# A hybrid decoder trunk on one core: seams between stages reordered, first weight tile ahead of x, a layer's first eight units over eight banks, per-layer gate kept in PSUM, output in four transfers

## The chip, the cores and the metric

One NeuronCore of a Trainium2 chip runs the whole program. The metric is the device time in microseconds from the first to the last instruction of one execution, the median over several runs.

## The reference

One inference step of two layers over 288 tokens (a prompt of 256, and 8 samples of 4), width 1024, all in float32. Each layer:

```python
z = rmsnorm(x, ln1) @ w_in                    # [u, v | B, C, xin | gate_A, gate_B], 7 x 1024
v = rmsnorm(gelu(v), ln_v)
ya = (gelu(u) * (tril(w_s[g]) @ v + b_s[g])) @ w_a
yb = (B * conv3_causal(C * xin)) @ w_b
x += (sigmoid(gate_A) * ya + sigmoid(gate_B) * yb) @ w_o
# PEER: q = rmsnorm(x, ln2) @ w_q; 8 heads, top 16 of 128 x 128 key pairs, softmax weights g
#   x += sum_k g_k * gelu(u_tab[eid_k] . h) * v_tab[eid_k]        over 16384 experts
x += sigmoid(rmsnorm(x, ln3) @ w_pg) * (pe @ w_ple)
```

At the end comes one more RMSNorm. Beside y, the outputs are the convolution state and the normalised v rows of the samples.

## The kernel before

**Units.** Activations lie feature-major: x is 8 chunks of 128 features by 288 tokens. Every weight comes from one stream of tiles [128, 1024] (512 KB); four tiles are a quad, and a layer has `QUADS` of them. One tile makes one unit: TensorE multiplies its 8 blocks of 128 x 128 with the 8 chunks of the operand and sums in one PSUM bank. Precision comes from a split in three: weight and operand are each a high part (fp32r) and a low part (the rest), and a unit has 8 x 3 = 24 matmuls (high x high, high x low, low x high; lines 1326 to 1328). The stages by their first quad are v, u, c, x, b, ga, gb (0 to 13), W_a (14), W_b (16), W_o (18), W_q (20), the expert table u (24, `Q_U`, 128 units on the prompt's 256 tokens), the table v (`Q_V`, 128 units), W_ple (one quad) and W_pg, the gate (two quads, `Q_PG`).

**Queues.** Each engine runs an order written out by hand, tied together by counting semaphores. SP issues the weight tiles into four buffers `raw`, and a tile's buffer is free when its low part was made (`lo`). ScalarE makes the high part (`split` in its block, line 463), VectorE the low part (`ahead`, line 832), both two units ahead of TensorE, since `w_hi` and `w_lo` have two buffers. In the expert stage for u GpSimd makes the low part in halves (line 380). So one late step holds the next-but-one unit.

**Banks.** A unit j of a quad writes bank j (0 to 3), and VectorE or ScalarE evacuates it (`evac`); TensorE waits for the bank's evacuation before the next quad's unit j. Bank 4 is for the sum of squares. Normalisation is applied late: the product is made from x times the gain, and `evacuate` (line 878) multiplies it with `root`, 1/rms of each token.

**Sums of squares.** ScalarE squares the chunks (line 444), GpSimd adds eight chunks with seven additions (`sum_chunks`, line 304), TensorE sums over the partitions with a float32 matmul of a matrix of ones (`sum_squares`, line 1316) after the second unit of the stage's first quad (`first_quad`), ScalarE takes the square root (`mean_root`, line 502, with a table load ahead at line 497) and VectorE the reciprocal (`inverse_root`, line 854). There are four in a layer, and one at the end.

**From W_b to W_o.** VectorE's loop evacuates a W_b unit into t_op (line 966), makes a weight low part (967), adds the other branch (969), and makes the operand's low part (971) after ScalarE's high part (607).

**Experts.** During the u units 0 to 63 (quads 0 to 15, `U_TOP` 13 and `U_ONLY` 3; `fine_segment`) VectorE picks the top 16 with sorts and makes `route`. TensorE transposes it after quad 14 (`rt_w`, `rT_ok`, lines 1446 to 1454). VectorE turns it into `routeT` (lines 1084 to 1096, `rT_in`); ScalarE waits for that ahead of quad 15 (line 655), and in quad 15 also writes ones to `mat` (`one_tiles`, line 646), whose end is `ones_ok`. For the last 64 units (`mixing_quad`) VectorE makes one-hot matrices of four tokens at a time (`matches`, `shared`, lines 1103 and 1110), ScalarE their low halves (`low_halves`, line 665), TensorE multiplies them (lines 1476, 1477) between the units' chunks, the first group after 21 of unit 0's 24 matmuls.

**The gate.** VectorE evacuates W_pg's product times root to `z[8 + c]`, ScalarE takes the sigmoid in place (line 774), VectorE multiplies with `z[c]` (1272), adds to x (1276) and, with ScalarE (`next_operand`), makes the next layer's operand (`next_lower`, line 871). Then all engines jump back to the head of the layer's loop.

**The end.** VectorE makes t_op in eight products (line 1304), and GpSimd sends y_out in two halves (line 429).

## Time and profile before

| | us |
|---|---|
| median of 3 runs | 2337.24 (2336.13 to 2341.18) |
| the profiled execution's own time | 2335.74 |
| its span, first to last instruction | 2334.2 |
| TensorE, matmuls busy | 2268.6 |
| VectorE busy | 1708.1 |
| ScalarE busy | 1390.2 |
| GpSimd busy | 875.9 |

The profile is of one execution. Its own time stands 1.5 us under the median. PE is TensorE's matmuls, PEld its weight loads, DVE VectorE, ACT ScalarE, POOL GpSimd and SP the queue that issues the weights. Matmuls overlap, so a busy time is the sum of overlapping stretches merged, and the distance from one start to the next says how fast they flow: 0.133 us for a matmul of 288 columns and 0.119 us for one of 256 in an undisturbed unit. A row of a timeline has its start, its length, engine, line, operation, output and inputs, shapes and count, and in brackets how long the engine had been idle before it and whose signal is taken to have ended that.

### The profile page before, as it was taken

What the parts mean: (1) busy time and instruction counts of PE and PEld (TensorE: products, weight loads), DVE (VectorE), ACT (ScalarE), POOL (GpSimd) and SP (SyncE); (2) the same over time, 40 slices, a digit from 0 to 9 for tenths busy, and PEclk for the clock granted to TensorE, in tenths of its full rate; (3) what the DMA queues carried; (4) which work ended last, traced back from release to release, by engine and by line L of the source; (5) the groups of instructions that cost most, each with busy time, mean ns of one, the idle gap of its engine ahead of it and who ended that gap; (6) DMA issues with size and microseconds to landing.
All of it is one profiled execution on the core that took longest, in us unless ns stands there. A gap on an engine that the chain in (4) does not pass through costs nothing.

```text
span 2334.2 us, 52338 instructions
## 1 busy us (share of the span) xinstructions
PE 2268.6 (97%) x15806; PEld 2103.0 (90%) x15806; DVE 1708.1 (73%) x3261; ACT 1390.2 (60%) x2712; POOL 875.9 (38%) x789
## 2 busy tenths in 40 slices
PE   7999999999999999999999999999999999999996
PEld 7989999998999888888899999999999998888885
DVE  5536768956888788788764467699378878888877
ACT  5544446666777555555654444566677775555555
POOL 3100007986777222111221001099877761211112
PEclk9999999999999999999999999999999999999998
DMA  5434454554444789788444345455444448888873
GB/s 185 155 121 170 158 182 153 183 180 160 156 159 154 254 294 321 268 298 279 165 156 155 119 166 182 134 185 185 165 160 159 155 158 285 295 311 278 295 255 102
DMA packets 126650, 460.77 MB, mean 197 GB/s; under 512 B 14672, under 2 KB 14864, under 8 KB 126032
## 3 DMA queue, kind: packets, MB, share of 16 engines
q1 hardware_dynamic: 105840, 384.02, 46.8%
q0 software_dynamic: 20704, 75.52, 11.5%
q8 instruction: 44, 0.72, 0.1%
q14 instruction: 62, 0.51, 0.1%
HBM read 455.53 MB, written 3.95 MB: 197 GB/s over the span
## 4 chain that ended last, share of the span: by engine, by line
PE 69%; POOL 11%; issue 11%; DVE 4%; ACT 2%; POOLq 1%; DVEq 0%; ACTq 0%; DMA 0%; SPq 0%
PE ps L1326 13%; PE ps L1328 12%; PE ps L1327 12%; POOL w_lo L380 11%; PE ps L1500 9%; PE ps L1502 9%; PE ps L1501 9%; PE ps L1476 1%; PE ps L1477 1%; ACT w_hi L463 1%; DVE w_lo L832 1%; DVE b_lo L871 1%; POOLq L306 1%; PE ps L1385 0%; ACT b_hi L506 0%
## 5 line engine op out<-in xcount | busy, mean ns | idle before, releaser
L1326 PE MATMUL ps<-h_hi,w_hi 128*128 128x256 f32 (+1 forms) x2592 | 752.2, 290 | 26.5 <-DVE w_lo L815 12.0
L380 POOL TENSOR_TENSOR w_lo<-raw,w_hi 128x512 fp32r<-128x512 f32 x508 | 649.2, 1292 | 281.9 <-ACT w_hi L485 153.0
L1327 PE MATMUL ps<-h_lo,w_hi 128*128 128x256 f32 (+1 forms) x2592 | 743.1, 287 | 0.0
L1328 PE MATMUL ps<-h_hi,w_lo 128*128 128x256 f32 (+1 forms) x2592 | 739.1, 285 | 0.0
L1326 PEld LDWEIGHTS ps<-h_hi,w_hi 128*128 128x128 f32 x2592 | 494.0, 191 | 30.2 <-issue 18.9
L1327 PEld LDWEIGHTS ps<-h_lo,w_hi 128*128 128x128 f32 x2592 | 493.4, 190 | 0.1
L1328 PEld LDWEIGHTS ps<-h_hi,w_lo 128*128 128x128 f32 x2592 | 490.9, 189 | 0.0
L463 ACT ACTIVATE w_hi<-raw 128x1024 fp32r<-128x1024 f32 x340 | 359.7, 1058 | 198.0 <-PE ps L1328 193.3
L1173 DVE TENSOR_TENSOR w_lo<-raw,w_hi 128x512 fp32r<-128x512 f32 x504 | 348.1, 691 | 127.8 <-ACT w_hi L703 86.0
L832 DVE TENSOR_TENSOR w_lo<-raw,w_hi 128x1024 fp32r<-128x1024 f32 x214 | 264.1, 1235 | 219.4 <-ACT w_hi L463 216.9
L1500 PE MATMUL ps<-w_hi,h_hi 128*128 128x512 f32 x1016 | 401.5, 395 | 0.0
L1502 PE MATMUL ps<-w_hi,h_lo 128*128 128x512 f32 x1016 | 400.0, 394 | 0.0
L1501 PE MATMUL ps<-w_lo,h_hi 128*128 128x512 f32 x1016 | 398.2, 392 | 0.0
L1326 PE MATMUL ps<-b_hi,w_hi 128*128 128x288 f32 x1152 | 345.5, 300 | 6.3 <-DVE w_lo L832 4.2
L1328 PE MATMUL ps<-b_hi,w_lo 128*128 128x288 f32 x1152 | 341.4, 296 | 0.0
L1327 PE MATMUL ps<-b_lo,w_hi 128*128 128x288 f32 x1152 | 336.2, 292 | 0.0
L703 ACT ACTIVATE w_hi<-raw 128x512 fp32r<-128x512 f32 x248 | 156.9, 633 | 199.6 <-PE ps L1502 192.7
L1502 PEld LDWEIGHTS ps<-w_hi,h_lo 128*128 128x128 f32 x1016 | 191.2, 188 | 45.4
L1501 PEld LDWEIGHTS ps<-w_lo,h_hi 128*128 128x128 f32 x1016 | 191.4, 188 | 43.9
L1500 PEld LDWEIGHTS ps<-w_hi,h_hi 128*128 128x128 f32 x1016 | 190.7, 188 | 43.4 <-issue 0.8
L1326 PEld LDWEIGHTS ps<-b_hi,w_hi 128*128 128x128 f32 x1152 | 216.4, 188 | 11.0 <-issue 5.2
L1327 PEld LDWEIGHTS ps<-b_lo,w_hi 128*128 128x128 f32 x1152 | 219.3, 190 | 0.3
(214 smaller groups left out, 3031.5 us busy)
## 6 DMA issues: line engine op xcount, KB each, us to landing
raw<-stream SPq DMA_DIRECT2D x730, 512.0 KB
x_keep<-x POOLq DMA_DIRECT2D x2, 1152.0 KB, 6.4
x<-x_keep POOLq DMA_DIRECT2D x2, 1152.0 KB, 10.3
x<-x_in SPq DMA_DIRECT2D x4, 288.0 KB, 3.9
y_out<-t_op POOLq DMA_DIRECT2D x2, 576.0 KB, 3.1
ws<-ws_in POOLq DMA_DIRECT2D x2, 512.0 KB, 3.6
ring<-u_rows,rows POOLq DMA_INDIRECT x44
ring<-stream,rows POOLq DMA_INDIRECT x42
```

The costliest lines, as they stand in the source:

```text
L306: pool.drain()
L380: return pool.tensor_tensor(w_lo[:, k % 2, lo_col:hi_col], raw[:, k, lo_col:hi_col], w_hi[:, k % 2, lo_col:hi_col].bitcast(F32), ALU.subtract)
L463: act.activation(w_hi[:, j % 2, :], raw[:, j, :], ACT.Copy).then_inc(hi, 1)
L703: act.activation(w_hi[:, k % 2, 0:D // 2], raw[:, k, 0:D // 2], ACT.Copy).then_inc(v_hi, 1)
L832: dve.tensor_tensor(w_lo[:, j % 2, :], raw[:, j, :], w_hi[:, j % 2, :].bitcast(F32), ALU.subtract).then_inc(lo, 1)
L1173: dve.tensor_tensor(w_lo[:, k % 2, at:at + D // 2], raw[:, k, at:at + D // 2], w_hi[:, k % 2, at:at + D // 2].bitcast(F32), ALU.subtract). ...
L1326: pe.matmul(out, wh, rhs_hi, start=first, stop=False)
L1327: pe.matmul(out, wh, rhs_lo, start=False, stop=False)
L1328: return pe.matmul(out, wl, rhs_hi, start=False, stop=last)
L1500: pe.matmul(out, m_up, wh, start=first, stop=False)
L1501: pe.matmul(out, m_up, wl, start=False, stop=False)
L1502: m = pe.matmul(out, m_low, wh, start=False, stop=last)
```

## The change

- SP issues the first weight tile ahead of x, the other three behind it; ScalarE runs a Copy on a spare element first, splits tile 0 ahead of the operand and tile 1 behind it; VectorE makes tile 0's low part ahead of the operand's low parts.
- `sum_chunks` adds six chunks (five additions). `sum_squares` multiplies three inputs with ones: the sum, and the last two squares. In a layer's first quad it stands after the third unit.
- The first eight units write the banks of `V_BANK` (0, 1, 2, 3, 5, 6, 7, 4); their evacuation and the steps of ScalarE and VectorE are written in a new order.
- W_b: the addition stands ahead of the weight's low part. W_q's first quad: the third tile's low part stands ahead of the second evacuation.
- The route is transposed after quad 13. ScalarE waits for the transposition alone ahead of quad 15, and makes group 0's low halves within quad 15, in its third step. VectorE makes the first one-hot matrices ahead of waiting for `ones_ok`. `share` is copied ahead of `rt_w`.
- The gate: VectorE scales the product in its bank, ScalarE's sigmoid and VectorE's multiplication stay there, x is added from there; the bank is given free by ScalarE at `next_operand`. The order of splits, gates and operand parts changes, and the tile for the next layer's second unit comes last.
- The output goes in four transfers from SP's queue.

```diff
--- before.py
+++ after.py
@@ -54 @@
...
+V_BANK = [0, 1, 2, 3, 5, 6, 7, 4]
@@ -210 @@
...
+scaled = sem("scaled")
@@ -270 @@
...
+    sp.dma_start(raw[:, 0, :], quads[0, 0]).then_inc(raw_in[0], 16)
...
-    for j in range(4):
+    for j in range(1, 4):
@@ -284 @@
...
+    for c in range(0, C, 2):
+        sp.wait_ge(t_ok, DEPTH * T_OPS + c + 2)
+        sp.dma_start(y_out[:, c:c + 2, :], t_op[:, c:c + 2, :]).then_inc(out_y, 16)
@@ -299 @@
...
-        for k in range(1, C):
+        for k in range(1, C - 2):
...
-            if k < C - 1:
+            if k < C - 3:
@@ -424 @@
...
-    for half in range(2):
-        pool.wait_ge(t_ok, DEPTH * T_OPS + (half + 1) * (C // 2))
-        pool.dma_start(y_out[:, half * (C // 2):(half + 1) * (C // 2), :],
-                       t_op[:, half * (C // 2):(half + 1) * (C // 2), :]).then_inc(out_y, 16)
...
-    pool.wait_ge(out_y, 32)
+    pool.wait_ge(out_y, 16 * C // 2)
@@ -444 @@
...
+    act.activation(spare[:, :], eps[:, :], ACT.Copy)
+    act.wait_ge(raw_in[0], 16)
+    act.activation(w_hi[:, 0, :], raw[:, 0, :], ACT.Copy).then_inc(hi, 1)
...
-    for j in range(2):
-        act.wait_ge(raw_in[j], 16)
-        act.activation(w_hi[:, j, :], raw[:, j, :], ACT.Copy).then_inc(hi, 1)
+    act.wait_ge(raw_in[1], 16)
+    act.activation(w_hi[:, 1, :], raw[:, 1, :], ACT.Copy).then_inc(hi, 1)
@@ -490 @@
...
-                        beside(i * 4 + j)
+                        beside(i * 4 + j, j)
@@ -529 @@
...
-        step(0, 0)
-        step(0, 1)
+        for n in range(3):
+            step(0, n)
         mean_root(1)
-        gelu(0)
-        gelu(1)
-        for j in (2, 3):
-            step(0, j)
-            gelu(j)
-        for j in range(4):
-            step(1, j)
-            gelu(4 + j)
+        for n in range(3, 8):
+            step(n // 4, n % 4)
+            gelu(n - 3)
+        for n in range(5, 8):
+            gelu(n)
@@ -647 @@
...
-        fine_segment(1, U_TOP - 1, lambda u: one_tiles(u + (KEYS - 4 * U_TOP), 1))
+        fine_segment(1, U_TOP - 1, lambda u, j: one_tiles(u + (KEYS - 4 * U_TOP), 1))
...
-        act.wait_ge(rT_in, L + 1)
+        act.wait_ge(rT_ok, L + 1)
...
-        fine_segment(U_TOP + U_ONLY - 1, 1,
-                     lambda u: one_tiles((u - (E_MIX - 4)) * below + E_MIX, below))
-        act.drain().then_inc(ones_ok, 1)
@@ -671 @@
...
-        low_halves(0, 0, range(GROUP))
+        def rest_of_ones(u, j):
+            if j == 2:
+                act.wait_ge(rT_in, L + 1)
+                low_halves(0, 0, range(GROUP))
+            one_tiles((u - (E_MIX - 4)) * below + E_MIX, below)
+        fine_segment(U_TOP + U_ONLY - 1, 1, rest_of_ones)
+        act.drain().then_inc(ones_ok, 1)
@@ -770 @@
...
-            emptied(4 * (Q_PG - KEYS // 4) + c)
-            act.activation(z[:, 8 + c, :], z[:, 8 + c, :], ACT.Sigmoid).then_inc(sig, 1)
+            act.wait_ge(scaled, L * C + (c + 1))
+            act.activation(ps[:, c % 4, 0:T], ps[:, c % 4, 0:T], ACT.Sigmoid).then_inc(sig, 1)
...
+            act.nop().then_inc(evac, 1)
...
+        step(Q_PG, 2)
...
-        for c in range(2, C):
-            step(Q_PG + c // 4, c % 4)
+        next_operand(0)
+        step(Q_PG, 3)
+        sigmoid(2)
+        next_operand(1)
+        step(Q_PG + 1, 0)
+        sigmoid(3)
+        sigmoid(4)
+        next_operand(2)
+        for c in range(5, C):
+            step(Q_PG + 1, c - 4)
@@ -804 @@
...
+    def first_lower(j):
+        dve.wait_ge(hi, j + 1)
+        dve.tensor_tensor(w_lo[:, j, :], raw[:, j, :], w_hi[:, j, :].bitcast(F32),
+                          ALU.subtract).then_inc(lo, 1)
+    first_lower(0)
...
-    for j in range(2):
-        dve.wait_ge(hi, j + 1)
-        dve.tensor_tensor(w_lo[:, j, :], raw[:, j, :], w_hi[:, j, :].bitcast(F32),
-                          ALU.subtract).then_inc(lo, 1)
+    first_lower(1)
@@ -878 @@
...
-        ahead(0, 0)
-        ahead(0, 1)
+        def first_v(n):
+            dve.wait_ge(mm, u0 + (n + 1))
+            dve.tensor_tensor(z[:, n, :], ps[:, V_BANK[n], 0:T], root[:, :], ALU.mult).then_inc(evac, 1)
+        for n in range(3):
+            ahead(0, n)
         inverse_root(1)
-        evacuate(0, 0, z[:, 0, :], root[:, :])
-        evacuate(0, 1, z[:, 1, :], root[:, :])
-        for n in range(2, 8):
-            evacuate(n // 4, n % 4, z[:, n, :], root[:, :])
-            ahead(n // 4, n % 4)
+        first_v(0)
+        ahead(0, 3)
+        first_v(1)
+        first_v(2)
+        ahead(1, 0)
+        first_v(3)
+        first_v(4)
+        for n in range(5, 8):
+            ahead(1, n - 4)
+            first_v(n)
@@ -964 @@
...
-                ahead(i + Q_B, j)
...
+                ahead(i + Q_B, j)
@@ -980 @@
...
+        ahead(Q_Q, 2)
         evacuate(Q_Q, 1, z[:, 1, :], root[:, :])
-        for j in (2, 3):
-            evacuate(Q_Q, j, z[:, j, :], root[:, :])
-            ahead(Q_Q, j)
+        evacuate(Q_Q, 2, z[:, 2, :], root[:, :])
+        evacuate(Q_Q, 3, z[:, 3, :], root[:, :])
+        ahead(Q_Q, 3)
@@ -1077 @@
...
+        dve.drain()
+        dve.tensor_copy(share[:, :], flat(route[:, 2, 0:S_BLOCKS, :]))
         dve.drain().then_inc(rt_w, 1)
-        dve.tensor_copy(share[:, :], flat(route[:, 2, 0:S_BLOCKS, :]))
@@ -1132 @@
...
-        dve.wait_ge(ones_ok, L + 1)
-        dve.sem_inc(passed, 1)
-        evacuated(Q_U + U_TOP + U_ONLY)
...
+        dve.wait_ge(ones_ok, L + 1)
+        dve.sem_inc(passed, 1)
+        evacuated(Q_U + U_TOP + U_ONLY)
+        dve.sem_inc(passed, 1)
@@ -1267 @@
...
+        def scale(c):
+            dve.wait_ge(mm, u0 + (Q_PG * 4 + c + 1))
+            dve.tensor_tensor(ps[:, c % 4, 0:T], ps[:, c % 4, 0:T], root[:, :], ALU.mult).then_inc(scaled, 1)
...
-            dve.tensor_tensor(z[:, 8 + c, :], z[:, 8 + c, :], z[:, c, :], ALU.mult).then_inc(plus, 1)
+            dve.tensor_tensor(ps[:, c % 4, 0:T], ps[:, c % 4, 0:T], z[:, c, :], ALU.mult).then_inc(plus, 1)
...
-            dve.tensor_tensor(x[:, c, :], x[:, c, :], z[:, 8 + c, :], ALU.add).then_inc(x_up, 1)
+            dve.tensor_tensor(x[:, c, :], x[:, c, :], ps[:, c % 4, 0:T], ALU.add).then_inc(x_up, 1)
@@ -1281 @@
...
-        for c in range(C):
-            evacuate(Q_PG + c // 4, c % 4, z[:, 8 + c, :], root[:, :])
-            if c >= 2:
-                ahead(Q_PG + c // 4, c % 4)
-            if c >= 1:
-                gate(c - 1)
-            if c >= 3:
-                next_lower(c - 3)
-            if c >= 1:
-                add_gated(c - 1)
+        scale(0)
+        scale(1)
+        ahead(Q_PG, 2)
+        gate(0)
+        add_gated(0)
+        scale(2)
+        gate(1)
+        add_gated(1)
+        next_lower(0)
+        for c in (3, 4):
+            scale(c)
+            ahead(Q_PG + c // 4, c % 4)
+            gate(c - 1)
+            add_gated(c - 1)
+            next_lower(c - 2)
+        for c in (5, 6):
+            scale(c)
+            gate(c - 1)
+            add_gated(c - 1)
+            ahead(Q_PG + c // 4, c % 4)
+            next_lower(c - 2)
+        scale(C - 1)
+        gate(C - 2)
+        add_gated(C - 2)
+        gate(C - 1)
+        add_gated(C - 1)
         next_lower(C - 3)
-        gate(C - 1)
         next_lower(C - 2)
-        add_gated(C - 1)
         next_lower(C - 1)
+        ahead(Q_PG + 1, 3)
@@ -1310 @@
...
-    def sum_squares(n, acc=0):
+    def sum_squares(n):
...
-        pe.matmul(ps[:, 4, 0:T], ones[:, :], sq[:, acc, :], start=True, stop=True).then_inc(ss_ok, 1)
+        pe.matmul(ps[:, 4, 0:T], ones[:, :], sq[:, 0, :], start=True, stop=False)
+        pe.wait_ge(sq_ok, n * C)
+        pe.matmul(ps[:, 4, 0:T], ones[:, :], sq[:, C - 2, :], start=False, stop=False)
+        pe.matmul(ps[:, 4, 0:T], ones[:, :], sq[:, C - 1, :], start=False, stop=True).then_inc(ss_ok, 1)
@@ -1346 @@
...
-                       order=range(C), until=(0, 0, 0, 0)):
+                       order=range(C), until=(0, 0, 0, 0), squares_at=1):
@@ -1358 @@
...
-                if j == 1 and squares is not None:
-                    sum_squares(L * NORMS + squares, order[0])
-        first_quad(0, 0, squares=1)
-        segment(1, 3)
+                if j == squares_at and squares is not None:
+                    sum_squares(L * NORMS + squares)
+        first_quad(0, 0, squares=1, squares_at=2)
+        for j in range(4):
+            pe.wait_ge(lo, u0 + (4 + j + 1))
+            if j == 3:
+                pe.wait_ge(evac, e0 + 5)
+            for c in range(C):
+                m = product(ps[:, V_BANK[4 + j], 0:T], j, c * P, h_hi[:, c, :], h_lo[:, c, :],
+                            c == 0, c == C - 1)
+            m.then_inc(mm, 1)
+        segment(2, 2)
@@ -1443 @@
...
-        fine_segment(0, U_TOP + U_ONLY - 1)
+        fine_segment(0, U_TOP + 1)
@@ -1451 @@
...
-        fine_segment(U_TOP + U_ONLY - 1, 1)
+        fine_segment(U_TOP + 1, U_ONLY - 1)
```

## Rows read from the trace of the kernel before

**Rows 1.** The page's busy times: engine, busy us (share) x instructions
```profile
PE 2268.6 (97%) x15806; PEld 2103.0 (90%) x15806; DVE 1708.1 (73%) x3261; ACT 1390.2 (60%) x2712; POOL 875.9 (38%) x789
```
**Rows 2.** Waits of PE, whole span: line <- releaser: total us, times, longest us
```profile
PE ps L1326 <- DVE w_lo L815: 12.0, 1, 12.0
PE ps L1316 <- POOL ext L304: 11.9, 3, 8.3
PE ps L1326 <- DVE w_lo L832: 7.5, 12, 1.5
PE ps L1476 <- ACT hot_a L665: 6.2, 2, 3.1
```
**Rows 3.** Windows: length, busy of PE, PEld, DVE, ACT, POOL, clock, DMA share, GB/s
```profile
1689.90:1693.30 3.40, 3.40 (x18) 3.40 (x17) 0.00 (x0) 2.45 (x5) 3.40 (x4) 0.50 0.46 153
1703.50:1707.00 3.50, 3.50 (x19) 3.50 (x19) 2.85 (x4) 2.59 (x7) 1.73 (x2) 0.51 0.42 162
```
**Rows 4.** Timelines of ACT and PE, from the start to unit 2
```profile
10.76 1.06 ACT L453 ACTIVATE w_hi<-raw 128x1024 fp32r<-128x1024 f32 x1 [0.23 <-DMA raw<-stream]
...
17.98 1.28 ACT L463 ACT_TABLE_LOAD   x1 [3.49 <-PE ps L1328]
...
17.24 0.35 PE L1326 MATMUL ps<-h_hi,w_hi 128*128 128x288 f32 x1
...
21.72 0.40 PE L1326 MATMUL ps<-h_hi,w_hi 128*128 128x288 f32 x1 [0.19 <-DVE w_lo L832]
```
**Rows 5.** Timeline of PE, layer 0's second sum of squares
```profile
75.44 0.65 PE L1316 MATMUL ps<-ext,ones 128*128 128x288 f32 x2
...
76.06 0.29 PE L1327 MATMUL ps<-b_lo,w_hi 128*128 128x288 f32 x1
```
**Rows 6.** Timeline of PE, last chunk of W_o's first unit, layer 0
```profile
269.44 0.29 PE L1328 MATMUL ps<-h_hi,w_lo 128*128 128x288 f32 x1
271.22 0.40 PE L1326 MATMUL ps<-h_hi,w_hi 128*128 128x288 f32 x1 [1.49 <-DVE h_lo L865]
```
**Rows 7.** Timeline of PE, W_q's second quad, layer 0
```profile
308.93 0.39 PE L1326 MATMUL ps<-b_hi,w_hi 128*128 128x288 f32 x1 [0.69 <-DVE w_lo L832]
```
**Rows 8.** Timelines of PE, DVE and ACT, quad 15 and the mixing stage's entry, layer 0
```profile
537.72 0.39 PE L1326 MATMUL ps<-h_hi,w_hi 128*128 128x256 f32 x1 [1.79 <-POOL w_lo L380]
...
545.82 1.23 DVE L1103 TENSOR_TENSOR hot_a<-ps,routeT 128x1024 f16<-128x1024 f32 x1 [10.51 <-ACTq L660]
...
548.81 1.28 ACT L665 ACTIVATE hot_a<-hot_a,routeT 128x128 f16<-128x128 f16 x4 [3.23 <-DVE hot_a L1110]
...
549.27 0.23 PE L1476 MATMUL ps<-hot_a 128*128 128x128 f16 x1 [3.08 <-ACT hot_a L665]
```
**Rows 9.** Groups by form: shapes, count | busy us, mean ns | idle before, releasers
```profile
L832 DVE TENSOR_TENSOR w_lo<-raw,w_hi 128x1024 fp32r<-128x1024 f32 x214 | 264.1, 1235 | 219.4 <-ACT w_hi L463 216.9 <-issue 0.3
...
L878 DVE TENSOR_TENSOR z<-ps,root 128x288 f32<-128x288 f32 x48 | 20.9, 453 | 14.6 <-PE ps L1328 14.0 <-issue 0.3
...
L871 DVE SCALAR_TENSOR_TENSOR h_lo<-x,gains,h_hi 128x288 fp32r<-128x288 f32 x16 | 13.0, 814 | 1.6 <-ACT h_hi L506 1.6
...
L1272 DVE TENSOR_TENSOR z<-z 128x288 f32<-128x288 f32 x16 | 7.2, 450 | 0.3
```
**Rows 10.** Timelines of POOL and PE, gate and layer's end, layer 0
```profile
1139.21 1.63 POOL L304 TENSOR_TENSOR ext<-ext 128x288 f32<-128x288 f32 x2 [0.20 <-issue]
...
1140.89 0.75 PE L1316 MATMUL ps<-ext,ones 128*128 128x288 f32 x2 [1.81 <-POOL ext L304]
...
1162.80 0.39 PE L1326 MATMUL ps<-h_hi,w_hi 128*128 128x288 f32 x1 [1.95 <-DVE z L878]
...
1168.62 0.40 PE L1326 MATMUL ps<-h_hi,w_hi 128*128 128x288 f32 x1 [1.21 <-DVE h_lo L871]
```
**Rows 11.** Timelines of ACT and POOL, the end
```profile
2323.69 0.50 ACT L794 ACTIVATE root<-ps,eps 128x288 f32<-128x288 f32 x1 [0.77 <-PE ps L1316]
...
2330.10 0.56 POOL L429 DMA_DIRECT2D y_out<-t_op  x1 [1.14 <-DVE t_op L1304]
```

## The prediction

> **What bounds the kernel now.** I read the page's busy times first, then TensorE's waits, then the granted clock, and only then the timelines around each wait. TensorE is busy 97% of the 2334.2 us span [rows 1]. Its work hardly changes here, so what can be won lies in the stretches in which it stands still. The waits [rows 2] say how little that is: 12.0 us before the first matmul, 11.9 us at three sums of squares (8.3 of them in the last one), 7.5 us in twelve waits for low weight parts (the longest, 1.5 us, at 28 us, before the fifth unit of layer 0), 6.2 us at the two entries to the mixing stage. The granted clock adds something that no wait shows: four stretches of 3.41 us inside the kernel run at half speed, beginning at 549.8, 1164.2, 1689.9 and 1703.5 us, two of which stand as rows [rows 3]. A matmul-filled stretch at half speed loses half its length, 1.7 us. Each began after TensorE had stood still for 2 us or more.
>
> The profiled execution took 2335.74 us with a span of 2334.2 us; the median of the runs shown is 2337.24 us, 1.5 us above it. The sum below is against the profiled execution, and is then put on the median. From no change, about 0.2% (4.7 us) can be told here.
>
> **Start.** The first weight tile (512 KB) now goes ahead of x. Until now the second tile's split waited for its transfer until 10.76, and TensorE began after 12.0 us, behind the first tile's low part [rows 2, 4]. With the tile first, I put its landing near 5.3 us; with 1.06 us for the high part and 1.23 us for the low one TensorE begins near 8.3 us. But the second tile lands no earlier, because the bytes ahead of it are the same; ScalarE then does eight squares, loads a table (1.28 us, behind the wait for unit 0's end, at 17.98 until now) and only then splits tile three. Until now, from that load to the start of unit 2 at 21.72 it took 3.74 us [rows 4]. ScalarE is free at 14.45, so unit 2 starts at 18.2: **3.5 us** earlier, though unit 1 has already ended near 17.1. That the slow first stretch (up to 17.24, [rows 4]) comes earlier too is in these numbers. Next is the fifth unit's wait of 1.5 us [rows 2]: it goes, as units 4 to 6 have banks 5, 6 and 7, and the split that it waited for stands ahead of the root. In its place come two more matmuls for the sum (below, 1.0 us) and the 0.2 us at 21.72 is gone. Total at unit 4: **-3.7 us**. Bounds: -2.0, if table load and split fall later, to -4.7, if the stall ahead of unit 2 is nil.
>
> **Sums of squares.** Each of the nine sums has two float32 matmuls more and two GpSimd additions fewer. One sum's two passes began at 75.44, and the second weight matmul behind it at 76.06, of whose 0.62 us the first weight matmul takes 0.133 [rows 5]: a float32 matmul of 288 columns costs 0.49 us, two more 0.98 us. At the second sum (v's square sum) of either layer nothing hides them, since the additions are long done: **+2.0 us** together. Lower bound 0.7 a sum, upper 1.3, from 0.33 and 0.65 us per matmul, half and all of the pair's recorded length [rows 5]. The others are counted in their places.
>
> **W_b to W_o.** The last chunk of the first W_o unit waits 1.49 us as the profile counts it, 1.65 us over the normal distance [rows 6]. VectorE evacuates, lowers a weight tile (1.23 us, [rows 9]), and only then adds. With the addition first, the path is evacuation 0.45, addition 0.45, then the tile, while ScalarE makes the high part, then 0.45: ready 3.0 us after the unit's end where 2.8 is needed. **-1.35 us a layer, -2.7 in all**; bounds -1.65 and 0 a layer.
>
> **W_q.** The wait of 0.69 us counted, 0.86 over the distance [rows 7], is for a tile behind three evacuations; it now stands ahead of two of them, and the sum's 0.98 us gives TensorE's needs more time still. So 0.86 goes and 0.98 comes: **+0.2 us in all**, bounds -0.5 and +1.0.
>
> **Into the mixing stage.** Until now TensorE turned the routes only after quad 14; VectorE worked on them for 5 us while ScalarE stood waiting for it, so quad 15's third unit began 1.79 us late at 537.72. Then VectorE's first comparisons waited for ScalarE's last ones tile (done 545.6), ScalarE's low halves began at 548.81 and TensorE stood 3.08 us until 549.27 [rows 8]. Now the turn comes a quad earlier (11.4 us), so everything that depends on it is done before quad 15, and the comparisons no longer wait for the tiles. Over the distances the two waits are 1.94 and 3.24 us. What is new is 1.2 us of low halves in ScalarE's third step of quad 15; until now it does a step in some 2.3 us of 2.85, so it falls behind by about 0.6 and the next half tile is still in time. GpSimd then does two gathers (2.3 us) and its next half tile comes some 0.3 us late. So -5.2 + 0.3 a layer. The half-speed stretches at 549.8, 1689.9 and 1703.5, which follow exactly these waits [rows 3], have no cause any more: -5.1. **-14.9 us in all.** Bounds: -19 would need the clock to gain elsewhere too; I take -16, and -7 if both layers keep half of the waits and two of the stretches.
>
> **Gate, layer's end, next layer.** The sum waits for GpSimd until 1140.89; its last two additions took 1.63 us from 1139.21 and are dropped [rows 10]. The sum starts 1.8 us earlier and takes 1.0 us longer: unit 2 gains 0.8. The root gains nothing, since ScalarE's split and table load alone take until 1141.68. Now each product stays in its bank until gate and addition are done. VectorE does scale, gate, add (0.45 each), a tile (1.23) and an operand part (0.81 on average, [rows 9]) per unit, 3.4 us with handing over, against 3.19 for TensorE's unit. Unit 4 waits 0.8 us for its bank, unit 7 0.5 to 1.4 us for its tile, so the quads end 0.8 to 1.5 us later than until now. In return the layer's last operands come earlier: eight squares and operands follow at once, where until now the last chunk came 1.21 us after need at 1168.62. At the layer's start TensorE idles about 2 us before 1162.80 [rows 10]. The profile names VectorE's evacuation there, but that ended 0.6 us before, and the interval looks like the jump back of the outer loop; I let it stand. From there: unit 0 without a stall, unit 1 0.3 to 0.7 us for its tile, unit 2 at 1171 to 1172 instead of 1174, and no bank wait at unit 4: **-1.9 us** between the layers, bounds +3 and -4.
>
> A rule against this part: by the Trainium skill (VectorE: DVE Perf Modes, The TRN2 errata) a VectorE operation from PSUM has 120 fixed cycles instead of 58. With 0.96 GHz, an estimate from that page gives 0.065 us more for each of some 24 operations a layer, so 3 us less gain. The trace has 453 ns for the product read from PSUM and 450 ns for the one in SBUF [rows 9], and the measurement decides: I charge nothing.
>
> **Tail.** After the last unit nothing hides anything. The last square comes 2 to 2.9 us earlier as VectorE's order ends with gate, addition and operand parts, and the addition chain after it (0.79 us) is gone; the table load for the root then leads. I take the root, at 2323.69 until now [rows 11], 3.0 us earlier. Reciprocal and eight products stay. The last output quarter goes from SP's queue instead of GpSimd's second half at 2330.10 [rows 11], half the bytes: 0.5 us. **-3.5 us**, bounds -1.5 and -5.
>
> **Sum:** -3.7 + 2.0 - 2.7 + 0.2 - 14.9 - 1.9 - 3.5 = -24.5 us. 2335.7 becomes 2311.2; on the median, 2312.7 us.
>
> **Rivals.** (a) As summed, 2312.7 us, chance 0.64; its own spread is 5 us. (b) The clock keeps its stretches: new waits (1.1 us ahead of unit 2, those for banks) bring as many as went, 5.1 us less gain: 2317.8 us, 0.12. For it speaks that in layer 1 the wait of 1.9 us was followed by one and in layer 0 the same wait by none; against it, that the new waits are shorter. (c) ScalarE is late in quad 15: ones tiles, low halves and splits then hold TensorE 2 to 3 us at each entry. 2318 us, 0.08. (d) VectorE becomes the bound of the gate's two quads, each of the last six units waiting 0.5 us in both layers, with the root's tail pushed along: 6 us, 2318.7 us, 0.08. (e) More than summed: no stall at unit 2, at the gate or at the loop: 2306 us, 0.05. (f) Slower: one mechanism, the clock in the first eight units of a layer. TensorE now starts before its operands keep up and stops again after two units. Should it be held at half speed there, a matmul costs 0.107 us more, a layer's eight units 20.5 us, both layers 41 us. Above 229 such matmuls (24.5 us), some 60% of these units, the change ends slower; wholly held, 2354 us. Nothing of the kind shows after the present stall at unit 4. 0.02. (g) The edits don't do what they say, the waits being the outer loop's jumps and loads: 2335 us, 0.01.
>
> **Numbers.** The likeliest gives 2312.7. (a) reaches from 2307 to 2318 and (b) to (d) lie near 2318 to 2319, with their own bounds to 2321; (e) reaches 2305. The range 2305 to 2321 leaves out the two rare cases and the ends, under 2 in 10. Faster by over 0.2% are (a) to (e), 0.97; within it 0.01; slower 0.02.
>
> **What would show it.** TensorE's first matmul near 8.3 us, unit 2 near 18.2, no wait of over 1 us at the fifth unit. Sums with six passes 0.245 us apart. No wait at the low halves, comparisons near 528 and not 545, three half-speed stretches fewer. In the gate, a wait for the bank of unit 4 and one for unit 7's tile. The root's last square root 3 us earlier after the last unit. Wrong would be the argument if the entry to the mixing stage still holds TensorE, or if the half-speed stretches only move.

## The result, and the profile after

The changed kernel takes 2307.43 us (median of 4 runs, 2306.84 to 2307.70) beside 2337.69 us of the kernel before on the same chip: ratio 0.9872, interval 0.986 to 0.9884, so 30.3 us less. The profiled execution takes 2306.84 us with a span of 2305.3 us; the span of before was 2334.2 us. The direction was forecast rightly, the range of 2305 to 2321 us holds the result, and the likeliest value, 2312.7 us, has 5.3 us too little gain.

The page's busy times and TensorE's waits, where [rows 1, 2] stand for before (waits: line <- releaser: total us, times, longest):

```profile
PE 2268.5 (98%) x15842; PEld 2103.2 (91%) x15842; DVE 1700.8 (74%) x3261; ACT 1390.3 (60%) x2713; POOL 858.3 (37%) x769
```
```profile
PE ps L1376 <- DVE h_lo L829: 7.9, 1, 7.9
PE ps L1376 <- DVE w_lo L848: 5.6, 8, 2.0
PE ps L1376 <- ACTq L782: 4.3, 3, 2.6
PE ps L1363 <- POOL ext L309: 3.0, 1, 3.0
PE ps L1376 <- POOL w_lo L385: 2.4, 4, 0.7
```

TensorE is busy as long as before: the sums have 36 matmuls more (18 pairs of 0.49 us, 8.8 us), against four half-speed stretches of 1.7 us loss each that went. So what the span lost is waiting. The first product waits 7.9 us instead of 12.0, the sums 3.0 instead of 11.9, and the two waits of 3.1 us for the low halves at the entry to the mixing stage are not in the list. New is the line of ScalarE's queue (L782, the count that frees a bank): 2.6 us of it is the jump of the outer loop, the other two are the gate's unit 4 in either layer.

To say where the 28.9 us of span went I compared the end of each unit's last product in the two traces; all rows of the table are such differences.

| stretch | predicted | measured |
|---|---|---|
| start, to the end of the fifth unit | -3.7 | -3.3 |
| second sums, both layers | +2.0 | +1.9 |
| last operand ahead of a first quad, four seams | 0 | -1.9 |
| W_b to W_o, both layers | -2.7 | -2.9 |
| W_q without its seam, both layers | +0.2 | 0.0 |
| into the mixing stage, both layers | -14.9 | -14.9 |
| gate of layer 0 to the fifth unit of layer 1 | -1.9 | -2.3 |
| gate of layer 1 | none of its own | +0.3 |
| after the last unit | -3.5 | -5.6 |

(Two drifts of 0.1 us make up the rest.)

At the start, the tile's split, the first product, and units 1 and 2, where [rows 4] had 10.76, 17.24 and 21.72; of each line the first column is the start in us, the second the length:

```profile
5.12 1.06 ACT L450 ACTIVATE w_hi<-raw 128x1024 fp32r<-128x1024 f32 x1 [2.29 <-DMA raw<-stream]
...
7.92 0.61 PE L1376 MATMUL ps<-h_hi,w_hi 128*128 128x288 f32 x1 [7.92 <-DVE h_lo L829]
...
14.53 1.28 ACT L466 ACT_TABLE_LOAD   x1
...
18.71 0.40 PE L1376 MATMUL ps<-h_hi,w_hi 128*128 128x288 f32 x1 [2.03 <-DVE w_lo L848]
```

For the first product and unit 2, 8.3 and 18.2 us were predicted; 7.92 and 18.71 came. The sum of squares behind the third unit is three pairs of passes, 0.49 us apart:

```profile
22.01 0.65 PE L1363 MATMUL ps<-ext,ones 128*128 128x288 f32 x2
22.50 0.65 PE L1365 MATMUL ps<-ext,ones 128*128 128x288 f32 x2
22.98 0.65 PE L1366 MATMUL ps<-ext,ones 128*128 128x288 f32 x2
```

At the entry to the mixing stage, where [rows 8] had the first hot product at 549.27 behind 3.08 us of waiting, ScalarE's low halves now come at 534.71 inside quad 15, and the product stands among the others without a wait. The window in which a half-speed stretch would lie shows the full clock (columns as in [rows 3]):

```profile
534.71 1.27 ACT L662 ACTIVATE hot_a<-hot_a,routeT 128x128 f16<-128x128 f16 x4
...
539.01 0.23 PE L1534 MATMUL ps<-hot_a 128*128 128x128 f16 x1
```
```profile
540.00:543.40 3.40, 3.40 (x33) 3.16 (x31) 3.00 (x5) 2.68 (x8) 2.91 (x4) 1.00 0.59 214
```

### The profile page after: what moved, and what is told of

Same layout as the page of the kernel before. It is cut to its first block, busy times and chain, and to the rows that moved or that the text cites. A ratio compares the mean times of both kernels' runs of the same rounds, so it can differ in the third digit from the quotient of the medians.

```text
span 2305.3 us, 52369 instructions
## 1 busy us (share of the span) xinstructions
PE 2268.5 (98%) x15842; PEld 2103.2 (91%) x15842; DVE 1700.8 (74%) x3261; ACT 1390.3 (60%) x2713; POOL 858.3 (37%) x769
## 4 chain that ended last, share of the span: by engine, by line
PE 78%; POOL 12%; issue 5%; ACT 2%; DVE 1%; POOLq 1%; DMA 0%; SPq 0%; DVEq 0%; ACTq 0%
PE ps L1376 15%; PE ps L1378 14%; PE ps L1377 14%; POOL w_lo L385 12%; PE ps L1558 10%; PE ps L1560 10%; PE ps L1559 10%; PE ps L1534 1%; PE ps L1535 1%; ACT w_hi L466 1%; DVE w_lo L848 1%; PE ps L1443 0%; PE ps L1445 0%; DMA raw<-stream 0%; PE ps L1447 0%
```

## The experiments

The differences below are against the kernel before as it ran beside each version on the same chip, so that versions from several chips can be set beside each other. The changed kernel stands at -30.3 us. The intervals of the ratios are about 0.0015 to either side (3.5 us), so small parts are read from the unit ends of the profiled executions. They repeat to some tenths away from the start, where transfers vary by 1 us.

**The entry to the mixing stage put back.** GpSimd's part doesn't change; TensorE, VectorE and ScalarE get the order before:

```
-                fine_segment(0, U_TOP + 1)
+                fine_segment(0, U_TOP + U_ONLY - 1)
                 pe.wait_ge(rt_w, L + 1)
...
+                dve.wait_ge(ones_ok, L + 1)
...
                 matches(0, 0)
...
-                fine_segment(U_TOP + U_ONLY - 1, 1, rest_of_ones)
...
+                low_halves(0, 0, range(GROUP))
```

> The changed kernel with the entry to the mixing stage put back (routes turned after quad 14, comparisons behind the ones tiles, low halves behind quad 15), the rest as changed. Theory: the two waits of TensorE return in each layer (about 1.9 and 3.2 us over the distances), and behind them two or three stretches at half speed of some 3.4 us, each worth 1.7 us: 13 to 16 us more than 2307.4, so 2320 to 2323. Rival one: the half-speed stretches went with another part of the change; then none shows and it is 9.5 to 10 us more, 2317. Rival two: ScalarE in quad 15 takes part of it back; then it is under 8 us more.

2319.13 us, -18.7: the part is worth 11.5 us here. By unit ends layer 0 loses 6.7 us and layer 1 5.3 us. The waits are those of before, but only layer 0 has a half-speed stretch; in layer 1 the same waits were followed by none:

```profile
PE ps L1528 <- ACT hot_a L665: 6.2, 2, 3.1
...
PE ps L1370 <- POOL w_lo L385: 5.0, 4, 1.8
```
```profile
543.76:547.16 3.40, 3.40 (x17) 3.40 (x18) 2.51 (x3) 2.41 (x6) 1.01 (x1) 0.50 0.57 214
...
1692.00:1695.40 3.40, 3.38 (x28) 2.86 (x29) 1.93 (x4) 3.10 (x9) 0.57 (x1) 1.00 0.79 294
```

So the waits are a fixed price, about 5 us a layer as summed, and a stretch after them is not. The theory's 13 us were too much for this one, and the first rival (no stretch) too little.

**The entry alone, on the kernel before** (the same edit the other way round).

> The kernel before with the entry to the mixing stage alone changed. Theory: the same 14 to 15 us come off, 2337.5 becomes about 2323; the stretches at 549.8, 1689.9 and 1703.5 go, the one at 1164.2 stays, since its wait is the outer loop's and not touched. Rival one: the stretches stay or move elsewhere, about 10 us off, 2327.5. Rival two: the parts depend on each other; then the gain here and the loss in the run that undoes it differ by over 2 us.

2322.47 us, -15.4. By unit ends 6.6 us come off in layer 0 and 8.3 in layer 1, 14.9 together. That is 2.9 us more than the run before gave (3.9 by medians), over the 2 us that the theory set for its second rival, that the parts depend on each other. By unit ends the difference is the stretches. In layer 0, with one in the kernel before and one in the run before, the two agree, 6.6 and 6.7 us; in layer 1, with two against none, they are 8.3 and 5.3. The waits themselves do not depend on the other edits; why fewer stretches follow them in one kernel than in the other is not shown. The stretch at the outer loop's jump stays (the row below), and one turned up at 2281.24 behind the wait for the gate's sum, where the kernel before had none:

```profile
1158.26:1161.60 3.34, 3.34 (x16) 3.34 (x15) 3.34 (x6) 0.87 (x2) 1.31 (x2) 0.50 0.46 157
```

**The sums with seven additions and one product again.**

```
-                for k in range(1, C - 2):
+                for k in range(1, C):
...
-                pe.matmul(ps[:, 4, 0:T], ones[:, :], sq[:, C - 2, :], start=False, stop=False)
-                pe.matmul(ps[:, 4, 0:T], ones[:, :], sq[:, C - 1, :], start=False, stop=True).then_inc(ss_ok, 1)
```

> The changed kernel with each sum of squares from one accumulated chunk again (seven GpSimd additions, one float32 product). Theory: six sums that stood in nobody's shadow give back 0.97 us each (5.8 us); against it VectorE's last low part ahead of the two first quads takes 0.95 instead of 0.45 us beside a GpSimd addition and TensorE waits 0.5 us more at each of four seams (2.0 us), and the gate's sum and the last sum come 0.3 to 1 us later. Net 2 to 4 us less than 2307.4, about 2304.5. Rival: the four seams shrank for another reason than the two additions that were dropped; then they stay short and it is 5 us less, 2302.5.

2309.11 us, -28.8: 1.5 us slower where 3 us faster was expected. The four executions lie in two pairs, near 2306.8 and 2311.2, and the profile is of the slowest. Up to the gate it went as expected: six sums give back 0.97 to 0.99 us each, and the four seams cost 0.50, 0.43, 0.52 and 0.44 us more. What I had put too low is the gate. Its sum again stands 1.81 us for GpSimd, and this distance of 2.1 us was followed by a half-speed stretch in layer 1; at the start another one began at 20.06 us. The pair of faster executions lists the higher granted clocks (0.997 and 0.998 against 0.996 and 0.995), which fits a different number of stretches in executions of one kernel.

```profile
1130.68 0.75 PE L1363 MATMUL ps<-ext,ones 128*128 128x288 f32 x2 [1.81 <-POOL ext L309]
```

The seam itself is seen in four lines, VectorE's eighth low part and GpSimd's addition beside it. First the kernel before, where TensorE's wait follows, then the changed one:

```profile
70.66 0.74 POOL L304 TENSOR_TENSOR ext<-ext 128x288 f32<-128x288 f32 x1 [2.19 <-ACT ext L550]
...
70.76 0.95 DVE L865 TENSOR_TENSOR b_lo<-t_op,b_hi  x1
...
71.77 0.40 PE L1326 MATMUL ps<-b_hi,w_hi 128*128 128x288 f32 x1 [0.51 <-DVE b_lo L865]
```
```profile
67.50 0.45 DVE L881 TENSOR_TENSOR b_lo<-t_op,b_hi  x1
```

The same subtraction takes 0.45 us alone and 0.95 us beside an addition that started first. By the Trainium skill (SBUF — State Buffer, SBUF: two separate sides) VectorE with two operands in SBUF and a GpSimd operation share a pair of ports, and who starts second stands fully blocked until the other is done. The trace agrees nearly: the addition ends at 71.40 and the subtraction at 71.71, 0.5 us after the 71.21 that it would need alone. Had it begun only at 71.40 it would have ended at 71.85, so by this estimate some 0.14 us of it did pass beside the addition.

**The first three sums of a layer with one product, the others as changed.**

```
-                sum_chunks(L * SQUARES)
+                sum_chunks(L * SQUARES, direct=0)
...
+                m = pe.matmul(ps[:, 4, 0:T], ones[:, :], sq[:, 0, :], start=True, stop=not direct)
+                if direct:
...
+                            sum_squares(L * NORMS + squares, squares not in (1, 2, 3))
```

> The changed kernel, but the first three sums of a layer from one accumulated chunk again (seven additions, one product), the gate's sum and the last one as changed. Theory: as the run with all sums undone, without its loss at the gate and at the end: 3.5 to 4.5 us less than 2307.4, about 2303.3. If the additions cost more at the seams than 0.5 us each, it is above 2304.5; if nothing, near 2301.6.

2305.60 us, -32.3, so 2.0 us less than the changed kernel where 4 were expected. The unit ends give -0.98 for each of the six sums, +0.5 for each of the four seams, as the theory had it, and what it lacked: about +0.25 each for the fifth unit and a tile of W_q, in both layers, that the longer sum had covered (1.0 us), and 1.3 us for a half-speed stretch behind the outer loop's jump, which the changed kernel's profile doesn't have. That the time lies above 2304.5 is these, and not dearer additions.

**The gate with products evacuated first, as before.**

```
-                    dve.wait_ge(mm, u0 + (Q_PG * 4 + c + 1))
-                    dve.tensor_tensor(ps[:, c % 4, 0:T], ps[:, c % 4, 0:T], root[:, :], ALU.mult).then_inc(scaled, 1)
...
+                for c in range(C):
+                    evacuate(Q_PG + c // 4, c % 4, z[:, 8 + c, :], root[:, :])
```

> The changed kernel with the gate's products evacuated to the working tile before sigmoid, product and addition, in the order of the kernel before; the sums stay at three products. Theory: the wait of 1.1 us for the bank of the gate's unit 4 goes in both layers, but the last operands come late again: the last chunk of the next layer's first unit waits about 1.2 us, the third unit starts later, and at the end the last square comes 2 to 3 us later after the last unit. Per layer change within 1 us, the end 2 us later: 2 to 3 us more than 2307.4, near 2310. Rival: the bank wait costs all that the earlier operands give, and the end is the sums' doing; then it is within 1 us of 2307.4.

2310.30 us, -25.6: 4.7 us slower than the changed kernel, the theory's side and more than its 3. The quads themselves are 0.4 us shorter in each layer without the bank wait. The next layer's first unit ends 1.7 us later, since its eighth chunk waits for the last operand part again (until 1154.60, with 0.62 us of idle time; the half-speed stretch ahead of it is covered by that wait), and the third unit comes a further 0.9 us later. The end is the large part: from the last unit's end to the root it takes 9.16 us instead of 5.82 and 5.96 in the changed kernel's two profiles, since TensorE's product of the eighth square waits for it:

```profile
2297.45 0.85 PE L1336 MATMUL ps<-ext,ones 128*128 128x288 f32 x1 [2.04 <-ACT ext L445]
```

**The first eight units over four banks.**

```
-                first_quad(0, 0, squares=1, squares_at=2)
+                first_quad(0, 0, squares=1)
+                segment(1, 3)
```

> The changed kernel with the first eight units over four banks again, the root behind the second unit and the evacuations in the order before; the first weight tile still goes ahead of x. Theory: the wait ahead of the fifth unit returns, 1.5 us in layer 0 and 0.9 in layer 1: 2309.8. Rival: with an earlier first unit the root is earlier too and the fifth unit no longer waits; then it is within 0.5 us of 2307.4, or even less, since the sum stands one unit earlier.

2305.22 us, -30.6, the same as the changed kernel: the rival's time came, though not by a wait that went. The wait ahead of the fifth unit is there again (0.47 us of idle time in layer 0, where before had 1.5; by unit ends 0.7 us in layer 0 and 1.2 in layer 1), and the sum goes back behind the second unit, into the wait for the third tile. With eight banks it stands behind the third unit, where nothing hides it: 1.46 us in each layer, all three products. Over the first five units, without the first one, four banks are 1.1 us faster in layer 0 and 0.3 us slower in layer 1.

```profile
25.50 0.40 PE L1374 MATMUL ps<-h_hi,w_hi 128*128 128x288 f32 x1 [0.47 <-DVE w_lo L851]
```

**Three parts at the ends put back**: x ahead of the first tile, W_b's tile ahead of the addition, the output in halves on GpSimd's queue.

```
-            sp.dma_start(raw[:, 0, :], quads[0, 0]).then_inc(raw_in[0], 16)
             for c in range(0, C, 2):
...
+                        ahead(i + Q_B, j)
                         dve.wait_ge(evac, L * EVACS + i * 4 + (4 * Q_B + j + 5))
...
-            for c in range(0, C, 2):
-                sp.wait_ge(t_ok, DEPTH * T_OPS + c + 2)
```

> The changed kernel with three parts put back that lie in stretches of their own, each read from its unit ends: x ahead of the first weight tile, in W_b the weight tile ahead of the addition, and the output in two halves on GpSimd's queue. Theory: the first part 2 to 4 us by the end of the fifth unit, the second 1.45 us in each layer (two more waits of 1.5 us ahead of W_o's last chunk), the third 1.0 to 1.7 us after the last product: 2314 to 2315. Rival to the first: the third unit starts by ScalarE's order and not by the weight's arrival, so that its start moves by less than 1 us and the sum is 2312.

2314.55 us, -21.3: 9.0 us slower than the changed kernel, where the theory had 6.6 to 7.6 (the absolute time fits only because the kernel before is 2 us faster on this chip). By unit ends the three parts are as expected: 2.9 us at the start, 1.46 and 1.45 us in W_b, and from the root to the end 10.2 us instead of 8.8, so 1.5 us for the output, 7.3 in all. The rest is two half-speed stretches of the profiled execution, one behind the jump (1.0 us) and one ahead of the last root (0.5 us).

```profile
PE ps L1374 <- DVE w_lo L821: 12.0, 1, 12.0
...
PE ps L1374 <- DVE h_lo L879: 3.0, 2, 1.5
```

**Two table loads brought forward.** The gate's bank wait looked like VectorE's chain. The timeline of the changed kernel says otherwise: behind the root ScalarE waits 2.00 us for TensorE ahead of the third tile's split, and loads the sigmoid's table only behind that. The new order did this itself. In the kernel before the first sigmoid stood ahead of that split, and its load lay in idle time, right behind the root (last two rows).

```profile
1130.19 0.48 ACT L505 ACTIVATE root<-ps,eps 128x288 f32<-128x288 f32 x1
1132.68 1.06 ACT L466 ACTIVATE w_hi<-raw 128x1024 fp32r<-128x1024 f32 x1 [2.00 <-PE ps L1378]
1133.76 1.28 ACT L778 ACT_TABLE_LOAD   x1
1135.05 0.70 ACT L778 ACTIVATE ps<-ps 128x288 f32<-128x288 f32 x2
...
1136.53 0.40 PE L1376 MATMUL ps<-b_hi,w_hi 128*128 128x288 f32 x1 [0.81 <-ACTq L782]
```
```profile
1142.20 1.28 ACT L774 ACT_TABLE_LOAD   x1
1144.74 0.81 ACT L774 ACTIVATE z<-z 128x288 f32<-128x288 f32 x2 [1.26 <-DVE z L878]
```
```
+                bring_table(ACT.Sqrt, 2)
                 for n in range(3):
                     step(0, n)
...
                 mean_root(4)
+                bring_table(ACT.Sigmoid, 3)
                 step(Q_PG, 2)
```

> The changed kernel with two table loads of ScalarE brought forward into time in which it stands idle: the sigmoid's directly behind the fourth root (now it runs 1.28 us after the third unit's weight split, ahead of the first sigmoid), and the square root's at the head of the layer loop (now a load of 1.28 us runs after the first unit's end, ahead of the third tile's split). Theory: the wait of 1.1 us for the bank of the gate's unit 4 goes in both layers, and the wait of 0.8 us ahead of the third unit of layer 1 shrinks to nothing, while in layer 0 ScalarE is busy with squares and nothing changes: 3 us less than 2307.4, 2304.4. Rival: VectorE's chain of scale, gate and addition is what keeps the bank; then the wait stays over 0.8 us and the time falls by 1 us at most.

2303.44 us, -32.4, 2.1 us less than the changed kernel by medians. By unit ends the quads of the gate are 0.6 us shorter in both layers and the third unit of layer 1 comes 0.9 us earlier; the bank wait is down to 0.24 us. So the theory holds, with 2.1 us for the three places together. The median's 2.1 us is the same figure partly by chance: in this profile one stretch behind the jump takes 1.5 us back, and the retrieval stage of layer 0 is 1.2 us shorter for a reason that isn't the loads (last section).

```profile
1128.76 1.28 ACT L500 ACT_TABLE_LOAD   x1
...
1130.75 1.06 ACT L466 ACTIVATE w_hi<-raw 128x1024 fp32r<-128x1024 f32 x1 [0.49 <-PE ps L1380]
1131.71 0.69 ACT L779 ACTIVATE ps<-ps 128x288 f32<-128x288 f32 x2
...
1134.03 0.40 PE L1378 MATMUL ps<-b_hi,w_hi 128*128 128x288 f32 x1 [0.24 <-ACTq L783]
```

A table load is 1.28 us in this trace, and the function starts right behind it (1133.76 + 1.28 is 1135.04). The Trainium skill (ScalarE: Activation LUTs, What ACT_TABLE_LOAD costs) has the same 1283 ns, and a drain of 1380 ns beside it that no load here shows.

**The changed kernel again, and two versions that take in what was learnt.**

> The changed kernel once more, unaltered, on the chip of the two that follow and as their measure. Theory: of its half-speed stretches none stands behind the entries to the mixing stage; behind the outer loop's jump back one may or may not stand, as it did in five of the seven kernels run so far that have the changed entry, so the time is 2306 to 2309 us.

2307.40 us, -30.3, with no stretch at the entries and, as in the changed kernel's first profile, none at the jump. (Of the eight kernels with the changed entry run before it, six have one there, not five of seven.)

The further edits of the faster version, beside the table loads and the single products of the first three sums:

```
+                    if k == C - 1 and behind is not None:
+                        pool.wait_ge(op_lo, behind)
...
+                if c in (1, 3):
+                    squares(c - 1)
+                    squares(c)
...
+                    pe.wait_ge(sq_ok, n * C - 1)
                     pe.matmul(ps[:, 4, 0:T], ones[:, :], sq[:, C - 2, :], start=False, stop=False)
+                    pe.wait_ge(sq_ok, n * C)
```

> The changed kernel with what the runs so far suggest: both table loads brought forward; a layer's first three sums from one accumulated chunk, with GpSimd's last addition held back until VectorE's eighth low part is done at the second and third; ahead of the layer loop four of the eight squares between the first operands; and in the other sums the product of the seventh chunk ahead of the wait for the eighth square. Theory: six times 0.97 us for the sums, nothing given back at the four seams (they stay under 0.4 us per distance), 2.5 to 4 for the tables, about 1 for the squares, 0.4 at the end: 9 to 11 us less than the changed kernel on the same chip, near 2297.5. Rival: the held addition is late for TensorE's sum at two units' distance; then the second and third sums wait 0.5 us or more and it is 2300.

2299.42 us, ratio 0.9838 (0.9824 to 0.9851): 8.0 us less than the changed kernel on the same chip and 38.3 less than the kernel before. It is the fastest of all. Sums 0.97 to 0.99 us each, seams unchanged: GpSimd's held addition starts behind the low part, which again takes 0.45 us.

```profile
66.05 0.45 DVE L888 TENSOR_TENSOR b_lo<-t_op,b_hi  x1
...
66.66 0.69 POOL L311 TENSOR_TENSOR ext<-ext 128x288 f32<-128x288 f32 x1 [2.91 <-DVE b_lo L888]
```

The missing 2 us are a stretch behind the jump and the start: the squares brought forward give the third unit only 0.6 us, since the second now waits for its tile.

> The same kernel as together, but the first eight units of a layer over four banks, as before the change. Theory: with the third tile no longer late, the eight banks are worth something: with four, the fifth unit waits 0.6 us in layer 0 and 1.1 in layer 1 for its bank, against 0.35 us of the sum that the eight banks leave uncovered in layer 0; 1 to 1.5 us more than together. Rival: the sum behind the second unit is still hidden by the wait for the third tile in both layers, as it was in the changed kernel with four banks (0.5 to 2 us less there); then it is the same or less than together.

2301.77 us, 2.4 us more than with eight banks. The theory holds in layer 1: with the tables in place the third tile is in time in layer 1, so its wait hides no sum any more, and the fifth unit waits, for its tile and not for its bank as I had written:

```profile
1164.23 0.40 PE L1384 MATMUL ps<-h_hi,w_hi 128*128 128x288 f32 x1 [1.17 <-DVE w_lo L858]
```

By unit ends this is 1.4 us in layer 1. Layer 0 is even, where 0.25 us was expected, and one stretch more, behind the last unit, brings the root 1.0 us later.

## Why the prediction was right, and what it missed

**Start.** Right within 0.5 us at every step, -3.3 us for -3.7. Three things in it balance less well than they look. The terms named for the first product, 5.3, 1.06 and 1.23, give 7.6 us and not 8.3; it came at 7.92, behind the first low part of the operand, which they leave out. The items up to the fifth unit (-3.5, -1.5, +1.0 and the 0.2 that went) give -4.2 and not -3.7. And the wait of 1.5 us at the fifth unit went, but the sum beside it was charged with two products, 1.0 us; it is three, 1.46 us, because the change moved it out of the wait for the third tile, where the first one had been hidden. That the eight banks earn nothing on their own here is shown by the run without them.

**Second sums, W_b, W_q.** 0.97 us a sum against 0.98, 1.45 a layer against 1.35 (the figures it gives, 1.65 less the 0.2 by which 3.0 exceeds 2.8, make 1.45), 0.0 against +0.2.

**The step that was missing: the seams, -1.9 us.** Sums of squares were costed by what they add on TensorE, and the two additions dropped on GpSimd counted as nothing but an earlier sum. They had slowed VectorE's last operand, on which TensorE waited at four places. The rows for it were in the trace of before; I had read [rows 9], where the last low parts of a layer average 814 ns (651 now), and used the number for the gate without asking what stood beside it.

**Into the mixing stage.** -14.9 us twice, and partly by luck. The waits, 5 us a layer, are confirmed by both runs. The three stretches at half speed, -5.1 us, need not follow the waits: with the same waits the run with the old entry had a single one, and the part was worth 11.5 us. They are no oddity of the profiled execution either: the seven executions of before beside that run list a granted clock of 0.992 or 0.993, the profiled one 0.994, and by medians the entry alone gave 15.4 us. Rival (b), that the stretches only move, is wrong at the entries: in none of the eleven profiles with the new entry does one stand behind them.

**Gate and layer's end.** -2.3 us for -1.9, by the forecast mechanism but other sizes. The predicted waits were 0.8 us for the bank of unit 4 (0.81 counted) and 0.5 to 1.4 us for unit 7's tile (none). But the first was put down to VectorE's 3.4 us a unit, which would make it a rate that can't be mended; it is a table load. And the gain hangs on the clock at the jump. In the kernel before, the stretch at 1164.2 cost nothing: behind it TensorE still stood idle for 1.21 us, until 1168.62, for the last operand part. VectorE makes that part by a chain of gates and additions of the layer before, which doesn't wait for the first unit:

```profile
1168.05 0.52 DVE L871 SCALAR_TENSOR_TENSOR h_lo<-x,gains,h_hi 128x288 fp32r<-128x288 f32 x1 [0.80 <-ACT h_hi L506]
```

In the changed kernel the part is in time, as predicted, and a stretch there is no longer hidden. Its two profiles have none; five variants with the new gate have one, and it costs them 1.0 to 1.5 us by the end of the first unit. With it the term would be about -1 us.

That VectorE works in PSUM costs next to nothing: 457 ns for the product of two operands with one in PSUM, 450 in [rows 9]; of the Trainium skill's 120 cycles against 58 (VectorE: DVE Perf Modes, The TRN2 errata) this kernel shows 7 ns.

```profile
L1304 DVE TENSOR_TENSOR ps<-ps,z 128x288 f32<-128x288 f32 x16 | 7.3, 457 | 1.0 <-ACT ps L778 1.0
```

**Tail, -5.6 us for -3.5, the term sized worst.** From the last unit's end to the root it took 9.67 us and takes 5.82: 3.9 us, not 3.0. Some 3.3 of it is the gate's new order (the run with the old gate). The rest, 0.5 us, would be the sum's, but isn't shown: the run with the old sums takes 6.24 us here, and runs whose end is as in the changed kernel take up to 6.3. The output was put at 0.5 us and is 1.5 to 1.7: I had costed the quarter's shorter transfer, and not that from issue to landing half the bytes on SP's queue take 2.1 us where GpSimd's took 3.1. Which part of that 1.0 us is the size and which the queue, no run here separates.

```profile
2296.58 0.50 ACT L808 ACTIVATE root<-ps,eps 128x288 f32<-128x288 f32 x1 [0.50 <-PE ps L1366]
```
```profile
y_out<-t_op SPq DMA_DIRECT2D x4, 288.0 KB, 2.1
```
```profile
y_out<-t_op POOLq DMA_DIRECT2D x2, 576.0 KB, 3.1
```

Seams 1.9, tail 2.1 and small terms make the 4.4 us by which the spans fell further apart than summed; the rest of the 5.3 us lies between profiled executions and medians. Rival (f), half speed in the first eight units, did not occur in the changed kernel; the run with the old sums has a single stretch there, at 20.06 us.

## What to carry to other kernels

Cost a dropped operation by its neighbours too: which engine shares its ports, and is the operation slowed beside it one that the bound engine waits for? Where a sum or another small job is moved, ask which wait hid it at its old place. And before a repeating wait is called an engine's rate, look in the timeline for a table load that stands between an idle stretch and the first use: here two lines ahead of idle time gave 2 us, and made the eight banks worth having. When an engine's order is rewritten, look where its table loads end up: the new order had itself moved one out of idle time, and the wait for unit 4's bank came with it.

## What was not expected of the hardware

A half-speed stretch (the granted clock at 1.2 instead of 2.4 GHz) is not a fixed consequence of a wait. In the thirteen profiles TensorE's products stood 2.0 us or more apart at 31 places ahead of the last unit; 17 were followed by a stretch of 3.41 us, 14 were not, and none of the thirteen distances between 1.5 and 1.9 us was. The same wait, in the same place, shows both. No profile here shows what decides it.

The quads of the retrieval stage take 11.413 us each in both layers of nine profiles, but 11.307 us in layer 0 of the other four (the entry, gate and banks put back, and the tables), spread over all their products. None of these edits touches the loop. It is worth 1.4 us in that layer (0.2 us of it is lost again behind the stage) and doesn't bear on the steps above, which are read outside it; it does stand in the spans of those four profiles. Its cause stays open.
